# x tiles and queries turned by full-width VectorE transposes and SBUF-to-SBUF DMAs in a hybrid attention layer

## What is computed

```python
h = rmsnorm(x, ln_gain)
q_a, k_a, v_a, g_a, b_c, c_c, x_c, g_c, q_m, g_m = split(h @ w_in)   # 1024,128,128,1024,4x512,512,512
o_a = swa_sink_attention(q_a, k_a, v_a, ...)  # 16 query heads of 64, 2 kv heads, chunks of 64, 128 keys,
                                              # QK-norm, relative bias, a sink per head
o_c = b_c * causal_conv3(c_c * x_c)           # 512 channels
o_m = memory_cross_attention(q_m, rmsnorm(mem) @ w_mem_kv, ...)  # 4 heads of 128, 256 memory tokens, QK-norm
mixed = concat(silu(g_a) * o_a, silu(g_c) * o_c, silu(g_m) * o_m)
out = x + mixed @ w_out
```

## Time and profile before

| | |
|---|---|
| time, median of 3 runs | 2826.0 us (2823.24 to 2828.24) |
| the profiled execution, its own time | 2824.71 us |
| its span, first to last instruction | 2822.9 us |
| TensorE matmuls busy | 2756.2 us, 98% |
| VectorE busy | 1390.3 us, 49% |
| ScalarE busy | 1018.9 us, 36% |
| GpSimd busy | 1286.5 us, 46% |
| mean DMA | 120 GB/s |
| mean granted TensorE clock | 0.997 |

### The profile page before, as it was taken

One profiled execution on the slowest core, in us unless ns is written; L12 is line 12 of the kernel. 1 busy time (PEld: TensorE's weight loads), 2 busy tenths in 40 slices (PEclk: granted clock), 3 DMA queues, 4 the chain that ended last, 5 costly groups with the idle time before them and its releaser, 6 DMA issues.

```text
span 2822.9 us, 37249 instructions
## 1 busy us (share of the span) xinstructions
PE 2756.2 (98%) x12859; PEld 2269.6 (80%) x12859; DVE 1390.3 (49%) x2419; ACT 1018.9 (36%) x2125; POOL 1286.5 (46%) x552
## 2 busy tenths in 40 slices
PE   6999999999999999999999999999999999999999
PEld 5888887888888888788888888788888888878887
DVE  5345575333525556614534557542534455753335
ACT  6333434333323343424332343433332234343333
POOL 4545543444444543344445454344444454434444
PEclk9999999999999999999999999999999999999999
DMA  6333333335533332334443333233453333333354
GB/s 213 113 93 102 113 101 98 109 127 168 167 96 99 97 120 94 102 101 152 164 143 98 106 97 112 90 112 112 154 175 119 90 98 112 101 100 107 126 170 142
DMA packets 215830, 337.94 MB, mean 120 GB/s; under 512 B 17702, under 2 KB 77172, under 8 KB 212852
## 3 DMA queue, kind: packets, MB, share of 16 engines
q1 hardware_dynamic: 194644, 283.49, 32.5%
q10 hardware_dynamic: 21024, 52.44, 5.4%
HBM read 293.13 MB, written 17.56 MB: 110 GB/s over the span
## 4 chain that ended last, share of the span: by engine, by line
issue 57%; POOL 40%; PE 1%; SPq 1%; POOLq 1%; DMA 0%; DVE 0%; ACT 0%; ACTq 0%
POOL w_lo L428 36%; POOL q_scale L434 2%; POOL early L442 1%; SPq L356 1%; POOLq L427 0%; DMA raw<-in_w_mem_kv 0%; POOL x_scale L434 0%; PE acc L1140 0%; PE acc L1142 0%; PE acc L1141 0%; POOL k_scale L434 0%; ACT w_hi L496 0%; SPq L358 0%; PE ps_t L1193 0%; POOLq L473 0%
## 5 line engine op out<-in xcount | busy, mean ns | idle before, releaser
L428 POOL TENSOR_TENSOR w_lo<-raw,w_hi 128x1024 fp32r<-128x1024 f32 x482 | 1176.8, 2441 | 1503.5 <-ACT w_hi L496 1503.5
L496 ACT ACTIVATE w_hi<-raw 128x1024 fp32r<-128x1024 f32 x482 | 509.7, 1057 | 1331.7 <-PE acc L1142 1308.9
L1140 PE MATMUL acc<-h_hi,w_hi 128*128 128x512 f32 x1792 | 706.4, 394 | 3.6 <-DVE ungated L1031 3.5
L1141 PE MATMUL acc<-h_lo,w_hi 128*128 128x512 f32 x1792 | 699.8, 391 | 0.0
L1142 PE MATMUL acc<-h_hi,w_lo 128*128 128x512 f32 x1792 | 699.4, 390 | 0.0
L1140 PE MATMUL acc<-w_hi,mix_hi 128*128 128x512 f32 x1088 | 428.1, 393 | 16.9 <-DVE stage L1125 9.4
L1141 PE MATMUL acc<-w_lo,mix_hi 128*128 128x512 f32 x1088 | 424.8, 390 | 0.0
L1142 PE MATMUL acc<-w_hi,mix_lo 128*128 128x512 f32 x1088 | 424.8, 390 | 0.0
L1140 PEld LDWEIGHTS acc<-h_hi,w_hi 128*128 128x128 f32 x1792 | 337.5, 188 | 81.3 <-DVE ungated L1031 4.2
L1142 PEld LDWEIGHTS acc<-h_hi,w_lo 128*128 128x128 f32 x1792 | 337.5, 188 | 71.1
L1141 PEld LDWEIGHTS acc<-h_lo,w_hi 128*128 128x128 f32 x1792 | 337.4, 188 | 68.3
(11 more groups left out here) (150 smaller groups left out, 2254.5 us busy)
## 6 DMA issues: line engine op xcount, KB each, us to landing
raw<-in_w_in SPq DMA_DIRECT2D x336, 512.0 KB, 3.7
raw<-in_w_out SPq DMA_DIRECT2D x130, 512.0 KB, 3.6
probs_t<-blocks_t SPq DMA_DIRECT2D x384, 64.0 KB, 2.1
xt<-in_x ACTq DMA_DIRECT2D x16, 1024.0 KB, 6.7
stage<-in_x ACTq DMA_DIRECT2D x64, 256.0 KB, 5.5
out<-stage ACTq DMA_DIRECT2D x64, 256.0 KB, 3.0
raw<-in_w_mem_kv SPq DMA_DIRECT2D x16, 512.0 KB, 7.8
ungated<-in_x SPq DMA_DIRECT2D x2, 1024.0 KB, 13.7
```

Of the source, the lines that this page charges most:

```text
L428: nc.gpsimd.tensor_tensor(w_lo[:, slot_mod % 2, :], raw[:, slot_mod, :], w_hi[:, slot_mod % 2, :].bitcast(F32), ALU.subtract).then_inc(lo_ ...
L496: nc.scalar.activation(w_hi[:, slot_mod % 2, :], raw[:, slot_mod, :], ACT.Copy).then_inc(hi_ready, 1)
L1140: nc.tensor.matmul(dst, st[0], mv[0], start=first, stop=False)
L1141: nc.tensor.matmul(dst, st[0], mv[1], start=False, stop=False)
```

## The change

The 32x32 blocks of x and of the queries are turned by instructions over all 128 partitions and then put into place by DMAs from SBUF to SBUF. For x, `x_flip` is one transpose of 128x2048, whose output lies in `flipped`; `move_x` on SP waits for it, after the last weights of the pass, and brings it back into xt with four DMAs, and x_high and x_low read xt, from slots 4 and 5 of the pass. For the queries, `turn_queries` writes into `stage` (one instruction for kind 0, four for kinds 1 and 2), and `move_queries` on SP copies it into `early`, four slots later in the table (slots 17, 29, 49), with 4, 8 and 8 DMAs. The queries then lie with the token outermost: the 128 columns of a unit are 8 elements apart for A, 16 for memory, and a row of A's scores is (query, half) instead of (half, query). Bias, sink and the reading of ps_o follow that order; the host reorders `sinks`. Waits on x_flipped and q_turned become waits on x_moved, x_free and q_moved.

```diff
-Q_TURN_AT = {FLOW0 + 1: (0, 0), FLOW0 + 2: (0, 1), FLOW0 + 13: (1, 0), FLOW0 + 14: (1, 1),
-             FLOW0 + 33: (2, 0), FLOW0 + 34: (2, 1)}
+Q_TURN_AT = {FLOW0 + 1: 0, FLOW0 + 13: 1, FLOW0 + 33: 2}
+Q_MOVE_AT = {s + 4: kind for s, kind in Q_TURN_AT.items()}
+Q_MOVED = (64, 192, 320)
...
-X_HIGH_AT = {5: (0, 1), 6: (2, 3)}
+X_HIGH_AT = {4: (0, 1), 5: (2, 3)}
...
-        flipped = nc.alloc_sbuf_tensor_at("flipped", [P, KT, P], F32, offset=flipped_at)
+        flipped = nc.alloc_sbuf_tensor_at("flipped", [P, 4, 512], F32, offset=flipped_at)
...
+            def move_queries(g, kind):
+                sp.wait_ge(q_blocked, g * 3 + kind + 1)
+                for i in range(4):
+                    if kind == 0:
+                        sp.dma_start(early[:, 12 + i, :], stage[32 * i:32 * i + 32, :, :]
+                                     ).then_inc(q_moved, 16)
+                    else:
+                        for part in range(2):
+                            sp.dma_start(early[64 * part:64 * part + 64, 4 * (kind - 1) + i, :],
+                                         stage[32 * i:32 * i + 32, 2 * part:2 * part + 2, :]
+                                         ).then_inc(q_moved, 16)
+            def move_x(tile):
+                sp.wait_ge(x_blocks, tile + 1)
+                for i in range(4):
+                    sp.dma_start(xt[:, 512 * i:512 * i + 512],
+                                 flipped[32 * i:32 * i + 32, :, :]).then_inc(x_moved, 16)
...
-            for half in range(2):
-                sp.dma_start(sink[64 * half:64 * half + 64, :],
-                             bass.AP(sinks.tensor, half, [[0, 64], [2, 8]]),
-                             allow_slow_non_contiguous=True).then_inc(c_dma, 16)
+            sp.dma_start(sink[:, :], bass.AP(sinks.tensor, 0, [[0, 64], [8, 2], [1, 8]])).then_inc(c_dma, 16)
...
-            for half in range(2):
-                for pair in range(8):
-                    sp.dma_start(bias[64 * half:64 * half + 64, pair, :],
-                                 bass.AP(bias_rows.tensor, (2 * pair + half) * CHUNK * ROW + CHUNK - 1,
-                                         [[ROW - 1, CHUNK], [1, KEYS]])).then_inc(bias_in, 16)
+            for pair in range(8):
+                sp.dma_start(bias[:, pair, :],
+                             bass.AP(bias_rows.tensor, 2 * pair * CHUNK * ROW + CHUNK - 1,
+                                     [[ROW - 1, CHUNK], [CHUNK * ROW, 2], [1, KEYS]])).then_inc(bias_in, 16)
...
                                 move_probs(g, MOVE_AT[at + s])
+                            if at + s in Q_MOVE_AT:
+                                move_queries(g, Q_MOVE_AT[at + s])
                             weights(s % 4, base + at + s, False,
                                     w_in[256 * s:256 * s + 256, c0:c0 + 512])
...
                                 w_out[256 * OUT_PAIRS[s]:256 * OUT_PAIRS[s] + 256, bass.ds(n * 512, 512)])
+                    move_x(g * TT + n)
...
             def x_load(i, src):
-                act.wait_ge(x_turned, 8 + 4 * TT)
-                act.wait_ge(x_flipped, i + 1)
+                act.wait_ge(x_free, 8 + KT + 4 * i)
                 act.dma_start(xt[:, :], src).then_inc(x_in, 16)
...
                 if q == 0:
-                    act.wait_ge(x_flipped, tile - TT)
+                    act.wait_ge(x_moved, (tile - TT - 1) * 64)
+                rows = xt[:, :].rearrange("p (i k a) -> p k i a", i=4, k=KT)
                 for j in range(4):
                     k = 4 * q + j
-                    hi = nc.scalar.activation(h_hi[:, k, bass.ds(n * P, P)],
-                                              flipped[:, k, :],
+                    hi = nc.scalar.activation(h_hi[:, k, bass.ds(n * P, P)].rearrange(
+                                                  "p (i a) -> p i a", i=4),
+                                              rows[:, k, :, :],
                                               ACT.Copy, scale=gain[:, k:k + 1])
...
             def gate_tanh(g, m, slots):
 
+                act.wait_ge(q_moved, g * Q_MOVED[2] + Q_MOVED[2])
...
-                    o = ps_o[:, :].rearrange("p (h e b q) -> p h b e q", h=2, e=2, b=4)
+                    o = ps_o[:, :].rearrange("p (e b q h) -> p h b e q", h=2, e=4, b=4)
                     for h in range(2):
                         cp = nc.scalar.activation(
                             ungated[64 * h:64 * h + 64, 4 * a:4 * a + 4, CHUNK * c:CHUNK * c + CHUNK
-                                    ].rearrange("p b (e q) -> p b e q", e=2),
+                                    ].rearrange("p b (e q) -> p b e q", e=4),
                             o[64:128, h], ACT.Copy)
...
             def x_flip(tile):
 
                 dve.wait_ge(x_scaled, tile + 1)
-                rows = xt[:, :].rearrange("p (k c) -> p k c", c=P)
-                for i in range(4):
-                    for j in range(4):
-                        last = nc.vector.transpose(
-                            flipped[32 * j:32 * j + 32, :, 32 * i:32 * i + 32],
-                            rows[32 * i:32 * i + 32, :, 32 * j:32 * j + 32])
-                last.then_inc(x_flipped, 1)
+                nc.vector.transpose(
+                    flipped[:, :, :].rearrange("p j (k a) -> p j k a", k=KT),
+                    xt[:, :].rearrange("p (k c j) -> p j k c", k=KT, j=4)).then_inc(x_blocks, 1)
 
             def x_low(tile, q, n):
                 dve.wait_ge(x_hi, tile * 4 + q + 1)
+                rows = xt[:, :].rearrange("p (i k a) -> p k i a", i=4, k=KT)
                 for j in range(4):
                     k = 4 * q + j
                     last = nc.vector.scalar_tensor_tensor(
-                        out=h_lo[:, k, bass.ds(n * P, P)], in0=flipped[:, k, :],
-                        scalar=gain[:, k:k + 1], in1=h_hi[:, k, bass.ds(n * P, P)].bitcast(F32),
+                        out=h_lo[:, k, bass.ds(n * P, P)].rearrange("p (i a) -> p i a", i=4),
+                        in0=rows[:, k, :, :], scalar=gain[:, k:k + 1],
+                        in1=h_hi[:, k, bass.ds(n * P, P)].bitcast(F32).rearrange(
+                            "p (i a) -> p i a", i=4),
                         op0=ALU.mult, op1=ALU.subtract)
...
-            def turn_queries(g, kind, part):
-                if part == 0:
-                    dve.wait_ge(q_normed, g * 3 + kind + 1)
-                rows = ungated[:, q_blocks(kind), :].rearrange("p t (b c) -> p t b c", c=P)
-                for i in range(4):
-                    for j in range(4):
-                        if kind == 0:
-                            cols = early[:, q_blocks(0), :].rearrange("p b (t q) -> p t b q", q=P)
-                            to = cols[32 * j:32 * j + 32, :, 2 * part:2 * part + 2,
-                                      32 * i:32 * i + 32]
-                        else:
-                            at, col = 64 * part + 32 * (j % 2), 64 * (j // 2) + 32 * (i % 2)
-                            cols = a_queries(kind - 1).rearrange("p b (t e) q -> p e t b q", e=2)
-                            to = cols[at:at + 32, i // 2, :, :, col:col + 32]
-                        last = nc.vector.transpose(
-                            to, rows[32 * i:32 * i + 32, :, 2 * part:2 * part + 2,
-                                     32 * j:32 * j + 32])
-                last.then_inc(q_turned, 1)
+            def turn_queries(g, kind):
+                dve.wait_ge(q_normed, g * 3 + kind + 1)
+                if kind:
+                    dve.wait_ge(q_moved, g * Q_MOVED[2] + Q_MOVED[kind - 1])
+                rows = ungated[:, q_blocks(kind), :]
+                if kind == 0:
+                    nc.vector.transpose(
+                        stage[:, :, :].rearrange("p j (a x) -> p j x a", a=32),
+                        rows.rearrange("p t (b c j) -> p j (t b) c", b=4, j=4)).then_inc(q_blocked, 1)
+                else:
+                    for part in range(2):
+                        for j in range(2):
+                            last = nc.vector.transpose(
+                                stage[:, 2 * part + j, :].rearrange(
+                                    "p (a h t b) -> p t b h a", a=32, h=2, t=TT),
+                                rows[:, :, 256 * part:256 * part + 256].rearrange(
+                                    "p t (b h c j) -> p j t b h c", b=2, h=2, j=2)[:, j])
+                    last.then_inc(q_blocked, 1)
...
-                hi = ps_o[0:64, :].rearrange("p (h e b q) -> p h b e q", h=2, e=2, b=4)
+                hi = ps_o[0:64, :].rearrange("p (e b q h) -> p h b e q", h=2, e=4, b=4)
                 for h in range(2):
                     o = ungated[64 * h:64 * h + 64, 4 * a:4 * a + 4, CHUNK * c:CHUNK * c + CHUNK
-                                ].rearrange("p b (e q) -> p b e q", e=2)
+                                ].rearrange("p b (e q) -> p b e q", e=4)
                     last = nc.vector.tensor_tensor(o, hi[:, h], o, ALU.add)
...
```

(30 more changed lines are left out.)

## The result

The changed kernel takes 2918.0 us (2914.9 to 2920.3, 4 runs), the kernel before 2826.2 on the same chip: ratio 1.0325, 95% interval 1.0311 to 1.0338, **92 us slower**. The prediction, 2834 with a range of 2809 to 2872, had the sign and missed the size.

The account below looks back on a forecast made before the run. TensorE, busy 2756.2 of 2822.9 us, was taken to set the pace, so only its waits or longer instructions count. The terms summed to +8 us, giving 2832.7, carried to the median as 2834; range 2809 to 2872.

Parts of the forecast that it names:

- boundary, L1125: Output projection boundaries: x_low ends ahead of the first bank, so TensorE's 15 waits on the output additions go, -14 us.
- x late: Last weight slot of each of 16 passes: x lands with 0.35 us margin, new wait taken as 0.3, +5 us.
- slot 49: 49th weight slot of a group: weights queue on SP behind A's second-half query DMAs; 4.0 us wait, four times, +16.
- slot 29: 29th weight slot of a group: weights queue behind A's first-half query DMAs; 0.8 us wait, four times, +3.
- slot 17: 17th weight slot of a group: weights behind memory-query DMAs land just in time; old wait of 1.17 goes, -5 us.
- strided loads: TensorE's scores: loading query columns 32 or 64 bytes apart stays near hidden under matmuls, +3 us (0 to 53).
- L1031: Drain of block B after the convolution: shorter VectorE transposes end TensorE's four waits on it, -4 us.
- PSUM reads: attention_out and attention_sum read PSUM at every second element; only the gate's chain shows it, +2 us.
- DMA traffic ahead of weights: Query moves at slots 17, 29 and 49: blocks in the same DMA queues add 0.2 to 0.3 us each, +3.
- The rival with 31 us: Scores on TensorE: strided stationary operand takes twice its 0.11 us step, 31 us more, 2862 us; chance 0.22.
- the 1.7 us of slack: Each weight slot: a w_hi on ScalarE may be 1.7 us late before TensorE has to wait.
- the rival built on it: Query transposes at 1.04 ns per element let the queue keep up: -14 us, 2812, or 2806; chance 0.23.

Follow-up runs that it names:

- the boundary alone: The kernel before with one table edit: all four quarters of x_high in slot 5 of the pass, none in slot 6; 2809.9 us, ratio 0.9943.

## Why the prediction was wrong, step by step

| step of the prediction | predicted us | measured us |
|---|---|---|
| transposes, each (in no sum) | 4.3 and 1.1 | 3.87 and 1.07 |
| boundary, L1125 | -14 | -15.5 (the boundary alone) |
| x late | +5 (16 x 0.3) | +33 (16 x 2.05) |
| slot 49 | +16 | +16 (3.6 to 4.6 listed, four times) |
| slot 29 | +3 | +4 (0.65 to 1.25, four times) |
| slot 17 | -5 | +6 (2.3 to 2.8, four times, less the old wait) |
| strided loads | +3 | +28 |
| L1031 | -4 | -4 |
| PSUM reads | +2 | 0 |
| DMA traffic ahead of weights | +3 | within the rows of the slots |
| start | -1 | -3 |
| clock at half speed | not in the sum | +23 |

The measured column adds up to about 87 of the 92; the rest was not assigned to a step.

**Three steps failed, and a fourth was missing.**

*The loads.* "I take +3, near hidden, as the matmuls and not the loads have set the steps so far." In the earlier trace rows the loads were listed with 187 ns while pairs of matmuls went in steps of 0.11 us: they were already longer than the steps that should have covered them, and that should have been read as no cover. Measured are +28 us. The rival with 31 us had the right mechanism and nearly the right size, and deserved the larger chance; the pair step of 0.236 us is also past the 0.2 that the prediction named as a sign of being wrong. The Trainium skill (Advanced Engine Details and Errata, Memory Cachelines) had spoken against the change, with its penalty for accesses that each go to another line of 16 bytes; the trace agrees with its direction, 187 to 332 ns.

*x's arrival.* "With 2 KB per partition in place of 512 bytes I add 0.5." The margin was 0.35 us, so all hung on this number, and I had scaled it from copies of a quarter of the size. It was 7.4 us and not 4.6. The page of the kernel before had a row of the right size, which I had not used, in its part 6:

```profile
xt<-in_x ACTq DMA_DIRECT2D x16, 1024.0 KB, 6.7
```

1 MB into the same tile, 6.7 us. As the upper bound it gives x at 627.5, past the 626 from which the prediction said the gain at the boundary would not hold. That condition was wrong in its turn: x came at what is 628 on the prediction's scale, and the waits on the additions went all the same, since TensorE's own 2 us of waiting give VectorE the time. In the changed kernel the additions wait for TensorE:

```profile
DVE stage L1146 <- PE acc L1163: 9.6, 14, 0.8
```

*Slot 17.* SP's four DMAs of 256 KB took 1.06 us each to issue, not the 0.6 of the 64 KB ones in the earlier trace rows, and the weights behind them stood 5.3 us after issue instead of 3.7. "Just in time" became 2.3 to 2.8 us late.

*The clock.* The sum had waits cost what they last, and put nothing for the clock, +23 us as measured. The change put in 24 waits of 1.7 to 4.6 us; 14 of them have a half-speed stretch at their end, 1.7 us more each, and two of those at slot 49 are double. Slot 49 alone gave 25 us where its waits are 16. The kernel before had shown such stretches behind its waits on L883.

**Right** were the transposes' durations and that 64-byte write steps add next to nothing, the waits at slots 49 and 29 to within a microsecond (at slot 49 shorter transposes, 3.8 us for 4.4, made up for slower issue and landing, so 4.00 to the digit is luck), the waits that go (L1125, L1031, the memory queries), and the unit in which all of it was counted, the 1.7 us of slack. The Trainium skill (Vector Engine (DVE) Microarchitecture Reference, The reshape front-end and per-opcode configuration) has a transpose at one element per cycle; the trace disagrees for these forms, 3868 ns for 2048 elements per partition being 1.9 ns each, where the narrow forms of the earlier trace rows take 1.04, so the rival built on it falls. Its other argument falls too: A's queries, read at 8-byte steps, took 1066 ns for 512, 2.1 ns each, no better than those at 16-byte steps.

## What to carry to other kernels

Where an engine loads one operand while it works on another, compare the two durations before calling the load hidden: if they are alike, a layout that slows the load can show nearly in full, as it did here (28 of 34.6 us). Price a transfer by the row whose size is nearest, not by the one whose route is. And before moving work off an engine that is not the bound, look for the one wait that it causes: here a table entry gave 15.5 us, and the rebuilding that had the same aim cost 92.

## What the runs showed of the hardware

- TensorE's stationary operand in float32, 64x128 with columns 32 bytes apart: loads listed with 332 ns instead of 187, pair step 0.236 us instead of 0.11. With 64 bytes between columns and matmuls of 256 columns behind it (190 to 304 ns) almost nothing showed.
- Reading PSUM at every second element costs nothing: L916 402 ns and L656 374, the same lines before 402 and 373.
- VectorE transposes of 128x2048, read at 16-byte steps: 3868 ns with contiguous writes, 3926 with 64-byte write steps. Read steps of 8 bytes are hardly better than 16 (1066 ns at 128x512 against 1106 in the earlier trace rows).
- TensorE's granted clock falls to 1.2 GHz for 3.4 us (once or twice over) behind waits: behind none of 15 listed with 1.67 us, 11 of 15 with 2.16, 15 of 15 with 3.19, with everything else alike but the copies that make the wait. A stretch of 3.4 us costs 1.7. In these 15 places the step from 2.16 to 1.67 us was worth 25.3 us, three times the waiting itself.
- A second queue for half of a copy made it arrive later (8.2 us against 7.5, medians of 16 passes); the weights' issue behind it had moved up too.
